# State-space sums in four row strips with a bank each, and means of q's squares as rows in four column strips

## The chip, the cores and the metric

One core of one Trainium2 chip (trn2) runs the kernel. The metric is the time of one execution on the device in microseconds, the median over several runs. The kernel drives five engines that run their own instruction streams and meet only at semaphores: TensorE (PE, matrix products into PSUM), VectorE (DVE), ScalarE (ACT), GpSimd (POOL) and SyncE (SP, which loads the weights). PSUM has eight banks of 128 partitions x 512 f32 here, `bank0` to `bank7`.

## The reference

Three blocks in a row work on x, 512 tokens of 1024 features. The first two are alike (attention over chunks, a convolution, retention, then an MLP of 4096). The third, the "second layer" of the names, has differential attention of 8 heads beside a state-space branch:

```python
xn = rmsnorm(h, norm1_gain[i])
proj = xn @ w_in[i]
q, k, v, u, gates = jnp.split(proj, splits, axis=-1)
q = rope(rmsnorm(q, q_norm_gain[i]), cos, sin)      # per head half of 64 features
k = rope(rmsnorm(k, k_norm_gain[i]), cos, sin)
...
# s5_layer: 32 groups of 16 channels, 64 complex states each
bu_re = jnp.einsum('blgc,gpc->blgp', uf, bb_re)
bu_im = jnp.einsum('blgc,gpc->blgp', uf, bb_im)
_, _, xr, xi = lax.associative_scan(_complex_affine_combine, (ar, ai, bu_re, bu_im), axis=1)
y = einsum(c_re, xr) - einsum(c_im, xi) + d_skip * uf
out = g * jax.nn.sigmoid(g @ w_glu + b_glu)         # g = gelu(y)
```

Only two parts of this third block matter here: the products that feed the scan of the states (sums over the channels), and the mean of the squares of q over each 64 features, which its norm needs.

## The kernel before

The residual x lies with features on partitions and tokens on the free axis. A weight matrix is streamed in units of 128 x 2048 values: SyncE loads a unit (`raw`), ScalarE rounds it to its high part (`w_hi`, line 1356), GpSimd makes the low part (`w_lo`, line 518), and TensorE does three products for each pair of tiles (high x high, high x low, low x high) at line 711. Two units are in flight at a time.

The projection of q and k in the second layer is cut into slots: one slot is 12 products of line 711 into one bank (0 to 3), and behind slot p TensorE runs `hook(p)`, small work for the state-space branch and the norms. Slots 0 to 15 make q (8 blocks of 128 features, two passes over four banks each), 16 to 31 make k, and v, the GLU and the projection follow. The other engines walk through the same numbers p in their own loops. The order is written out by hand in tuples of slots at lines 1270 to 1286. No planner moves anything: an engine does its instructions in this order and waits where a semaphore is not there yet.

The work that the change and the prediction touch:

- `sums_in(blk)` (line 999), hooks 8, 12, 16 and 20, for the four blocks of 128 channels. For each strip q of 32 partitions it multiplies `b_pow` by `uT`, over four sub-steps j and for a real and an imaginary part: 32 f32 products of 32 x 128 by 128 columns. The real part goes to bank 4, the imaginary part to bank 5, strip q to the columns q*128 of both. In a round r the real part takes strip r and the imaginary part strip r+1, so two strips are at work at once; three times per block TensorE waits until both strips are done (`strip_done`), so that no bank is written from two strips together.
- DVE, `states(blk, stage)` (line 2333), slots given by `STATES_AT`: stage 0 turns the sums (four reads of banks 4 and 5) and frees the two banks, stage 1 scans, stage 2 turns back and makes `state_ready`. It waits for tables that GpSimd makes (`turned`).
- `sums_out(blk)` (line 1017), hooks 14, 18, 22 and 26: products with `taps` (line 1024), then, when the state is ready, with the tables `ctab` (line 1031), all into bank 6, which DVE's `skip(blk)` reads and frees one slot later.
- `short_response` (line 987), hook 10: 32 products of line 995 into bank 6. ScalarE copies them to `taps` (line 1723).
- `q_columns(n)` (line 1035), hooks 9 and 17, for blocks 0 to 3 and 4 to 7 of q: the squares of q are the stationary operand, 128 tokens at a time, and two columns of `blk64` are the moving one, 16 products of 128 x 128 by 2 columns into bank 7. Tokens come out on partitions. DVE's `q_columns` (line 2376) adds the epsilon and frees bank 7; in slot 18 ScalarE and in slot 20 DVE (`column_root`) make the inverse root.
- In the same slots ScalarE takes q and k out of banks 0 to 3 with their squares (lines 1680 and 1682), and issues the DMAs that fetch each block's rotated partner, four per block (`fetch_partner`, line 1692, slots `PARTNER_AT`); DVE rotates (`rotate`, lines 2398 to 2401, slots `ROTATE_AT`: two blocks each in slots 8, 12, 16 and 20).
- `k_mean(j)` (lines 1051 and 1052, slots `K_AT` from 22 on) uses bank 7 in the same way for k, with ScalarE's `inverse_root` and DVE's `k_norm` behind it.

In DVE's loop one slot runs `skip`, then `states`, then its small jobs (rotations first). In ScalarE's loop it runs the next high part of weights (every fourth slot), the emptying of a bank, `short_response`, then the jobs, `fetch_partner` first.

## Time and profile of the kernel before

| what | value |
|---|---|
| median of 3 runs | 2146.66 us (2142.12 to 2146.75) |
| the profiled execution | 2144.72 us, its span 2142.9 us, granted clock 0.99 |
| TensorE products, busy | 2100.7 us, 98% of the span |
| VectorE / ScalarE / GpSimd busy | 1061.5 / 876.3 / 925.4 us |
| lines 1010 and 1041, the long forms of the change | 20.7 and 9.0 us busy |
| chain that ended last | PE 75%, issue 16%, POOL 3%, DVE 3% |

The span is what the profiler saw between the first and the last instruction; the time of the execution is 1.8 us longer. A f32 product leaves two records of TensorE, a product of line 711 one. "Granted clock" 1.00 is TensorE's full clock of 2.4 GHz, 0.50 the lower level of 1.2 GHz. Starts are in us from the start of the span. An engine that shows busy time beside another one's may still be what that one waits for: the timelines tell, not the shares.

### The profile page before, as it was taken

The page shows a single profiled execution, that of the slowest core. Times are in us where ns is not written, and L with a number is a line of the kernel's source. Part 1 is how long each engine was busy: PE and PEld are TensorE (multiplying, and loading weights), DVE is VectorE, ACT ScalarE, POOL GpSimd, SP SyncE. Part 2 cuts the span into 40 slices and gives each one's busy share as a digit, 9 for nine tenths or more (in the row PEclk, how much of TensorE's full clock was granted, in tenths as well). Part 3 has the DMA queues.
Part 4 walks back from the last instruction along what each step waited for, and adds up shares of the span by engine and source line. Part 5 has one row for each costly group of instructions (what it writes and reads, how often), then busy time and mean ns, then how long its engine had stood idle before and what let it go on. Part 6 is the DMA issues. An engine that isn't in the chain of part 4 may idle for free.

```text
span 2142.9 us, 27507 instructions
## 1 busy us (share of the span) xinstructions
PE 2100.7 (98%) x10200; PEld 1676.2 (78%) x10200; DVE 1061.5 (50%) x1725; ACT 876.3 (41%) x1219; POOL 925.4 (43%) x306
## 2 busy tenths in 40 slices
PE   8999999999999999999999999999999899999999
PEld 7875888888888776888888888877766787888887
DVE  5866242222247654422222258985588534554555
ACT  5345462223243445533222343164566534333332
POOL 5522444443455333545654456333312254444442
PEclk9999999999999999999999998899999999999999
DMA  5431213223224331233222242223111232322232
GB/s 182 150 117 71 77 63 98 97 98 98 99 69 149 125 93 46 79 99 98 94 100 87 92 148 85 66 84 108 60 60 60 95 100 81 97 88 90 97 98 78
DMA packets 120050, 202.29 MB, mean 94 GB/s; under 512 B 6544, under 2 KB 51856, under 8 KB 119696
## 3 DMA queue, kind: packets, MB, share of 16 engines
q1 hardware_dynamic: 112992, 189.12, 26.7%
q10 hardware_dynamic: 6960, 11.88, 1.9%
q8 instruction: 60, 0.98, 0.2%
q14 instruction: 38, 0.31, 0.0%
HBM read 189.44 MB, written 8.12 MB: 92 GB/s over the span
## 4 chain that ended last, share of the span: by engine, by line
PE 75%; issue 16%; POOL 3%; DVE 3%; ACT 1%; ACTq 1%; DMA 0%; POOLq 0%; DVEq 0%; SPq 0%
PE bank L711 63%; PE bank L813 5%; POOL w_lo L518 3%; PE bank L822 1%; PE bank L1010 1%; PE bank L765 1%; PE bank L840 1%; PE bank L880 1%; PE bank L774 1%; PE bank L868 0%; ACTq L1572 0%; DVE pr L2018 0%; PE bank L1041 0%; ACTq L1692 0%; PE bank L906 0%
## 5 line engine op out<-in xcount | busy, mean ns | idle before, releaser
L518 POOL TENSOR_TENSOR w_lo<-raw,w_hi 128x2048 fp32r<-128x2048 f32 (+1 forms) x167 | 741.9, 4442 | 1119.3 <-ACT w_hi L1356 1119.3
L711 PE MATMUL bank<-act_hi,w_hi 128*128 128x512 f32 x1488 | 595.6, 400 | 5.9 <-DVE hid L2561 2.5
L711 PE MATMUL bank<-act_hi,w_lo 128*128 128x512 f32 x1488 | 584.7, 393 | 0.0
L711 PE MATMUL bank<-act_lo,w_hi 128*128 128x512 f32 x1488 | 584.1, 393 | 0.0
L1356 ACT ACTIVATE w_hi<-raw 128x2048 fp32r<-128x2048 f32 (+1 forms) x170 | 314.2, 1848 | 591.2 <-PE bank L711 545.8
L711 PEld LDWEIGHTS bank<-act_hi,w_hi 128*128 128x128 f32 x1488 | 282.5, 190 | 78.0 <-issue 11.8
L711 PEld LDWEIGHTS bank<-act_hi,w_lo 128*128 128x128 f32 x1488 | 281.9, 189 | 60.7
L711 PEld LDWEIGHTS bank<-act_lo,w_hi 128*128 128x128 f32 x1488 | 282.5, 190 | 58.2 <-issue 1.4
L711 PE MATMUL bank<-h_hi,w_hi 128*128 128x512 f32 x704 | 277.7, 394 | 0.3 <-DVE x L2526 0.3
L711 PE MATMUL bank<-h_lo,w_hi 128*128 128x512 f32 x704 | 277.4, 394 | 0.0
L711 PE MATMUL bank<-h_hi,w_lo 128*128 128x512 f32 x704 | 277.4, 394 | 0.0
L2263 DVE TENSOR_TENSOR f<-f,bank 128x512 f32<-128x512 f32 x128 | 88.1, 688 | 238.7 <-PE bank L711 238.7
L2249 DVE SCALAR_TENSOR_TENSOR hid<-bank,rrow 128x512 f32<-128x512 f32 x64 | 43.7, 691 | 250.3 <-PE bank L711 245.3
L711 PEld LDWEIGHTS bank<-h_hi,w_hi 128*128 128x128 f32 x704 | 131.7, 187 | 33.4 <-DVE h_lo L2080 0.7
L711 PEld LDWEIGHTS bank<-h_hi,w_lo 128*128 128x128 f32 x704 | 131.7, 187 | 32.7
L711 PEld LDWEIGHTS bank<-h_lo,w_hi 128*128 128x128 f32 x704 | 131.7, 187 | 32.1
L2556 DVE TENSOR_TENSOR bank<-bank,rrow 128x512 f32<-128x512 f32 x44 | 30.7, 699 | 142.9 <-PE bank L711 140.4
L813 PE MATMUL bank<-act_hi,w_hi 128*128 128x512 f32 x192 | 76.3, 398 | 5.7 <-DVE act_lo L1940 5.2
L534 POOL TENSOR_TENSOR sums<-sums,squares 128x512 f32<-128x512 f32 x50 | 64.6, 1292 | 37.4 <-ACT squares L1374 35.1
L1993 DVE SCALAR_TENSOR_TENSOR bank<-ypad,lcol,bank 128x512 f32<-128x512 f32 x116 | 76.6, 755 | 0.0
L813 PE MATMUL bank<-act_hi,w_lo 128*128 128x512 f32 x192 | 74.8, 390 | 0.0
L813 PE MATMUL bank<-act_lo,w_hi 128*128 128x512 f32 x192 | 74.8, 389 | 0.0
(362 smaller groups left out, 2638.5 us busy)
## 6 DMA issues: line engine op xcount, KB each, us to landing
raw<-in_w_up SPq DMA_DIRECT2D x32, 1024.0 KB, 5.4
raw<-in_w_down SPq DMA_DIRECT2D x32, 1024.0 KB, 5.0
raw<-in_w_in SPq DMA_DIRECT2D x26, 1024.0 KB, 5.1
raw<-in_w_up SPq DMA_DIRECT2D x44, 512.0 KB, 4.6
raw<-in_w_in SPq DMA_DIRECT2D x28, 768.0 KB, 4.5
raw<-in_w_out SPq DMA_DIRECT2D x12, 1024.0 KB, 5.0
raw<-in_w_down SPq DMA_DIRECT2D x22, 512.0 KB, 4.2
raw<-in_w_attn_proj SPq DMA_DIRECT2D x4, 1024.0 KB, 5.1
```

The costliest lines, as they stand in the source:

```text
L518: pool.tensor_tensor(m.w_lo[slot][:, 0:n], m.raw[slot][:, 0:n], m.w_hi[slot][:, 0:n].bitcast(F32), ALU.subtract).then_inc(s["split_ready"], 1)
L534: ins = pool.tensor_tensor(m.sums[:], m.sums[:], m.squares[n % 4][:], ALU.add)
L711: mm = pe.matmul(o, ll if i == 2 else lh, rl if i == 1 else rh, start=first and n == 0, stop=last and n == len(steps) - 1)
L765: mm = pe.matmul(bank[b][:, t:t + 1], x[:, t * P:(t + 1) * P], m.per_d, start=(part == 0), stop=(part == 1))
L774: mm = pe.matmul(bank[b][:, t * P:(t + 1) * P], column[:, t:t + 1].to_broadcast([P, P]), m.ident, start=True, stop=True)
L813: mm = pe.matmul(bank[b][:], (wl if i == 2 else wh)[:, k % KU, cols], (m.act_lo if i == 1 else m.act_hi)[:, k, :], start=(k == 0 and i == ...
L822: pe.matmul(bank[b][:] if o is None else o, lhsT, rhs, start=True, stop=True).then_inc(s[f"full{b}"], 1)
L1356: act.activation(m.w_hi[slot][:, 0:n], m.raw[slot][:, 0:n], ACT.Copy).then_inc(s["w_hi"], 1)
L1993: ins = dve.scalar_tensor_tensor(to, y, w, sums, ALU.mult, ALU.add)
L2249: dve.scalar_tensor_tensor(m.hid[:, b, :], bank[b][:], 0.0, m.rrow[:], ALU.max, ALU.mult).then_inc(s[f"free{b}"], 1)
L2263: dve.tensor_tensor(sums, sums, bank[4 + b][:], ALU.add).then_inc(s[f"free{4 + b}"], 1)
L2556: dve.tensor_tensor(bank[b][:], bank[b][:], m.rrow[:], ALU.mult).then_inc(s["up_scaled"], 1)
```

## The change

`sums_in` now has four banks, 4 to 7, one for each strip, allocated as one tensor `quad`. The real part of strip q goes to columns 0 to 127 of bank 4+q, the imaginary part to columns 128 to 255. Four products of four different strips follow each other, and the waits for `strip_done` are gone. DVE's step 0 reads the four banks with one instruction for each of its four turns and frees all four at its end; one of these turns is now waited for.

The means of q's squares are made in two steps. `q_rows(n)` (hooks 10 and 18) takes 32 columns of `blk64` as the stationary operand and the squares as the moving one: four products of 512 columns, each to its strip of 32 partitions of bank 7. ScalarE copies the bank to `q_rows` in SBUF. `q_columns(n)` (hooks 11 and 19, instead of 9 and 17) turns that by four products with picked columns of the identity. `COLUMN_ROOT_AT` goes from 18 to 20. The number of f32 products falls from 2 x 16 to 2 x (4 + 4) there and stays 4 x 32 in `sums_in`.

```diff
--- before.py
+++ after.py
@@ -188,7 +188,9 @@
 
     with ExitStack() as ctx:
         m = memory(nc)
-        m.bank = [ctx.enter_context(nc.psum_tensor(f"bank{i}", [P, T], F32)) for i in range(8)]
+        m.bank = [ctx.enter_context(nc.psum_tensor(f"bank{i}", [P, T], F32)) for i in range(4)]
+        m.quad = ctx.enter_context(nc.psum_tensor("bank4", [P, 4, T], F32))
+        m.bank += [m.quad[:, i, :] for i in range(4)]
         m.x_park = nc.dram_tensor("x_park", (P, NT * D), F32, kind="Internal").ap()
         m.bias_table = nc.dram_tensor("bias_table", (DEPTH, 6, P * N_BIAS), F32, kind="Internal").ap()
         s = {name: ctx.enter_context(nc.semaphore(name)) for name in SEMAPHORES}
@@ -227,7 +229,7 @@
     "bias_loaded",
     "table_loaded",
     "x_parked", "x_back",
-    "taps_clear", "u_ready", "strip_done", "spread", "kernel_made", "glu_done",
+    "taps_clear", "u_ready", "spread", "kernel_made", "glu_done",
     "arena_free",
     "w_loaded0", "w_loaded1",
     "w_hi",
@@ -370,6 +372,7 @@
     m.partner = [ar(f"partner{i}", [P, T], 68 + 2 * i) for i in range(2)]
     m.q_root = [ar(f"q_root{i}", [P, T], 72 + 2 * i) for i in range(2)]
     m.q_mean, m.q_power = (ar(name, [P, 2, 8, NT], 72 + 2 * i) for i, name in enumerate(("q_mean", "q_power")))
+    m.q_rows = ar("q_rows", [P, T], 92)
     m.g_hi, m.g_lo = (ar(f"gated{i}", [P, 4, T], 76 + 8 * i, F32R) for i in range(2))
     m.uT = put("uT", [P, 4, T], at=late_at)
     m.ssm = ar("ssm", [P, KD, T], 40)
@@ -998,21 +1001,18 @@
 
     def sums_in(blk):
 
-        fill(4)
-        fill(5)
+        for b in QUAD:
+            fill(b)
         if blk == 0:
             pe.wait_ge(s["u_ready"], 4)
             pe.wait_ge(s["param_dve"], N_PARAM_B)
-        for r in range(4):
+        for part in range(2):
             for j in range(SUB):
-                for part in range(2):
-                    q = (r + part) % 4
-                    mm = pe.matmul(bank[4 + part][:, q * P:(q + 1) * P], m.b_pow[strips[q], SUB - 1 - j, part, blk, :],
+                for q, b in enumerate(QUAD):
+                    mm = pe.matmul(bank[b][:, part * P:(part + 1) * P], m.b_pow[strips[q], SUB - 1 - j, part, blk, :],
                                    m.uT[strips[q], blk, j * N_SUB:(j + 1) * N_SUB], start=(j == 0), stop=(j == SUB - 1))
-                    if j == SUB - 1:
-                        mm.then_inc(s["strip_done" if r < 3 else f"full{4 + part}"], 1)
-            if r < 3:
-                pe.wait_ge(s["strip_done"], c.up("strip_done", 2))
+                    if part == 1 and j == SUB - 1:
+                        mm.then_inc(s[f"full{b}"], 1)
 
     def sums_out(blk):
 
@@ -1032,14 +1032,20 @@
                                    start=False, stop=(part == 1), skip_group_check=True)
         mm.then_inc(s["full6"], 1)
 
-    def q_columns(n):
+    def q_rows(n):
 
         pe.wait_ge(s["q_squared"], c.up("q_squared", 4))
         fill(7)
         for j in range(4):
-            for t in range(NT):
-                mm = pe.matmul(bank[7][:, 0:8 * NT].rearrange("p (c j t) -> p c j t", c=2, t=NT)[:, :, j, t], m.q_square[j][:, t * P:(t + 1) * P],
-                               m.blk64.rearrange("p (c d) -> p c d", c=2)[:, :, 0], start=True, stop=True)
+            mm = pe.matmul(bank[7][strips[j], :], m.blk64.rearrange("p (c d) -> p c d", d=4)[:, :, 0], m.q_square[j][:], start=True, stop=True)
+        mm.then_inc(s["full7"], 1)
+
+    def q_columns(n):
+
+        fill(7)
+        for t in range(NT):
+            mm = pe.matmul(bank[7][:, 0:8 * NT].rearrange("p (c j t) -> p c j t", c=2, t=NT)[:, :, :, t], m.q_rows[:, t * P:(t + 1) * P],
+                           m.ident.rearrange("p (j c d) -> p c j d", j=4, c=2)[:, :, :, 0], start=True, stop=True)
         mm.then_inc(s["full7"], 1)
 
     def k_mean(j):
@@ -1061,6 +1067,8 @@
                 sums_in(blk)
             if p == SUMS_OUT_AT[blk]:
                 sums_out(blk)
+        for n in jobs_at(p, ROWS_AT):
+            q_rows(n)
         for n in jobs_at(p, COLUMNS_AT):
             q_columns(n)
         for j in jobs_at(p, K_AT):
@@ -1267,7 +1275,8 @@
     return x[:, 0, :], x[:, 1, :]
 
 
-COLUMNS_AT, COLUMN_ROOT_AT = (9, 17), 18
+QUAD = (4, 5, 6, 7)
+ROWS_AT, COLUMNS_AT, COLUMN_ROOT_AT = (10, 18), (11, 19), 20
 K_AT = (22, 24, 26, 28, 30, 36, 38, 42)
 PARTNER_AT = (6, 7, 10, 10, 14, 15, 18, 18, 21, 22, 24, 26, 29, 34, 36, 40)
 ROTATE_AT = (8, 8, 12, 12, 16, 16, 20, 20)
@@ -1703,6 +1712,8 @@
 
         for j in jobs_at(p, PARTNER_AT):
             fetch_partner(j)
+        for n in jobs_at(p, ROWS_AT):
+            evac(7, m.q_rows[:])
         for n in jobs_at(p, COLUMNS_AT):
             use(7)
         if p == COLUMN_ROOT_AT:
@@ -1739,7 +1750,7 @@
         if p == SHORT_AT:
             short_response()
         if p in SUMS_IN_AT:
-            use(4, 5)
+            use(*QUAD)
         if p in SUMS_OUT_AT:
             use(6)
         jobs(p)
@@ -2336,16 +2347,18 @@
         sin, cos = m.sin_n[blk % 2][:], m.cos_n[blk % 2][:]
         if stage == 0:
             dve.wait_ge(s["turned"], blk + 1)
-            full(4)
-            full(5)
-            dve.tensor_tensor(w0, bank[4][:], cos, ALU.mult).then_inc(s["dve_step"], 1)
-            dve.tensor_tensor(w2, bank[4][:], sin, ALU.mult).then_inc(s["free4"], 1)
+            for b in QUAD:
+                full(b)
+            re, im = (m.quad[:, :, part * P:(part + 1) * P] for part in range(2))
+            by_strip = lambda x: x.rearrange("p (q n) -> p q n", q=4)
+            dve.tensor_tensor(by_strip(w0), re, by_strip(cos), ALU.mult).then_inc(s["dve_step"], 1)
             c.up("dve_step")
-            link(dve.tensor_tensor(w1, bank[5][:], sin, ALU.mult))
+            dve.tensor_tensor(by_strip(w2), re, by_strip(sin), ALU.mult)
+            link(dve.tensor_tensor(by_strip(w1), im, by_strip(sin), ALU.mult))
             link(dve.tensor_tensor(w0, w0, w1, ALU.add))
-            dve.tensor_tensor(w1, bank[5][:], cos, ALU.mult).then_inc(s["free5"], 1)
-            freed(4)
-            freed(5)
+            link(dve.tensor_tensor(by_strip(w1), im, by_strip(cos), ALU.mult))
+            for b in QUAD:
+                dve.sem_inc(s[f"free{b}"], 1)
             link(dve.tensor_tensor(w1, w1, w2, ALU.subtract))
         if stage == 1:
             for q in range(4):
@@ -2412,6 +2425,8 @@
 
         for j in jobs_at(p, ROTATE_AT):
             rotate(j)
+        for n in jobs_at(p, ROWS_AT):
+            use(7)
         for n in jobs_at(p, COLUMNS_AT):
             q_columns(n)
         if p == COLUMN_ROOT_AT + 2:
```

## Rows read from the trace of the kernel before

**Rows 1.** The page of the kernel before, its first part: busy time of each engine.

```profile
PE 2100.7 (98%) x10200; PEld 1676.2 (78%) x10200; DVE 1061.5 (50%) x1725; ACT 876.3 (41%) x1219; POOL 925.4 (43%) x306
```

**Rows 2.** Windows: length, busy us of each engine (instructions), granted clock, DMA share, GB/s.

```profile
1290.00:1405.00 115.00, 113.89 (x901) 93.83 (x900) 101.53 (x125) 28.23 (x38) 59.69 (x30) 0.88 0.25 74
...
1302.60:1307.40 4.80, 4.80 (x14) 3.80 (x13) 4.77 (x2) 0.00 (x0) 4.80 (x3) 0.54 0.11 17
...
1319.00:1324.50 5.50, 5.50 (x24) 4.34 (x24) 2.89 (x5) 2.37 (x4) 0.00 (x0) 1.00 0.15 36
...
1357.40:1362.00 4.60, 4.60 (x12) 3.60 (x13) 4.53 (x4) 0.00 (x0) 4.44 (x4) 0.54 0.25 61
```

**Rows 3.** Timeline of TensorE, 1296 to 1407: start, length, line, operation, records.

```profile
1296.73 5.93 PE L1010 MATMUL bank<-uT,b_pow 32*128 32x128 f32 x64
...
1307.48 4.15 PE L1041 MATMUL bank<-cmat,q_square 128*128 128x2 f32 x32
...
1316.89 2.09 PE L995 MATMUL bank<-ctab,braw 128*32 128x128 f32 x64
...
1324.58 4.92 PE L1010 MATMUL bank<-uT,b_pow 32*128 32x128 f32 x64
...
1335.00 2.39 PE L1024 MATMUL bank<-uT,taps 128*128 128x128 f32 x20
...
1352.57 4.80 PE L1041 MATMUL bank<-cmat,q_square 128*128 128x2 f32 x32
...
1371.98 6.08 PE L1010 MATMUL bank<-uT,b_pow 32*128 32x128 f32 x64
...
1389.66 1.12 PE L1051 MATMUL bank<-q_square,cmat 128*128 128x512 f32 x2
...
1405.99 1.52 PE L1031 MATMUL bank<-state,ctab 128*32 128x128 f32 x48
```

**Rows 4.** Line 1010: what ended TensorE's idle time before it (us, times).

```profile
  PE bank L1010: 3.6, 12
```

**Rows 5.** Timeline of VectorE (DVE), 1299 to 1405; in brackets its idle time before.

```profile
1299.65 0.86 DVE L2398 TENSOR_TENSOR partner<-partner,rope 128x512 f32<-128x512 f32 x1 [3.59 <-DMA partner<-q]
...
1301.15 4.91 DVE L2401 TENSOR_TENSOR q<-q,partner 128x512 f32<-128x512 f32 x1
...
1310.70 0.69 DVE L2341 TENSOR_TENSOR w<-bank,cos_n 128x512 f32<-128x512 f32 x1
...
1313.34 0.69 DVE L2346 TENSOR_TENSOR w<-bank,cos_n 128x512 f32<-128x512 f32 x1
...
1325.61 0.69 DVE L2398 TENSOR_TENSOR partner<-partner,rope 128x512 f32<-128x512 f32 x1 [3.65 <-DMA partner<-q]
...
1328.18 0.69 DVE L2398 TENSOR_TENSOR partner<-partner,rope 128x512 f32<-128x512 f32 x1 [0.55 <-DMA partner<-q]
...
1334.53 0.69 DVE L2341 TENSOR_TENSOR w<-bank,cos_n 128x512 f32<-128x512 f32 x1
...
1338.86 5.25 DVE L2355 TENSOR_TENSOR_SCAN w<-par,w 128x128 f32<-128x128 f32 x8
...
1361.50 0.69 DVE L2341 TENSOR_TENSOR w<-bank,cos_n 128x512 f32<-128x512 f32 x1
...
1382.70 0.69 DVE L2341 TENSOR_TENSOR w<-bank,cos_n 128x512 f32<-128x512 f32 x1
...
1387.23 2.63 DVE L2355 TENSOR_TENSOR_SCAN w<-par,w 128x128 f32<-128x128 f32 x8
...
1404.26 0.69 DVE L2366 TENSOR_TENSOR state<-state,w 128x508 f32<-128x508 f32 x1
```

**Rows 6.** Timeline of ScalarE (ACT), around hook 10; ACTq is its issuing of DMAs.

```profile
1319.13 2.44 ACT L1723 ACTIVATE taps<-bank 32x512 f32<-32x512 f32 x4 [18.27 <-PE bank L995]
1321.68 5.01 ACTq L1692 DMA_DIRECT2D partner<-q  x8
```

**Rows 7.** Timeline of GpSimd (POOL): the low parts of one unit of weights.

```profile
1328.78 5.17 POOL L518 TENSOR_TENSOR w_lo<-raw,w_hi 128x2048 fp32r<-128x2048 f32 x1 [14.33 <-ACT w_hi L1356]
```

## Prediction

> **What bounds the kernel now.** I read the page first. TensorE is busy for 98% of the span [rows 1], so a change that makes its work shorter looks like a gain of the same size. That is an average, so I then read the stretch that the change touches, second layer, hooks 8 to 26, 1290 to 1405 us: by the windows its granted clock is 0.88 against 1.00 around it, TensorE is busy for 113.9 of 115 us and VectorE (DVE) for 101.5 [rows 2]. Next the timeline of TensorE in it: four `sums_in` of 4.9 to 6.1 us and two `q_columns` of 4.2 and 4.8 us [rows 3]. Last the timelines of DVE, ScalarE and GpSimd [rows 5 to 7]. The reader is to see there that DVE works nearly without a gap from 1299.65 to 1405: it idles 3.65 and 0.55 us for partners of q [rows 5], and in those 105 us does the rotations of q and the three steps of `states` for four blocks, in an order written out by hand. The last of these, the state of block 3, is done at 1404.95 (1404.26 and 0.69), and the products of `sums_out(3)` that read it start at 1405.99 [rows 3, 5]. So TensorE is 98% busy, and DVE is one microsecond behind it at the end of this stretch. What TensorE saves ahead of 1405 is worth about 1 us unless DVE gets shorter too.
>
> **What TensorE saves by itself.** A slot of 12 `L711` products takes 2.75 us at full clock (24 in 5.5) and 4.6 to 4.8 in windows at a mean clock of 0.54 [rows 2].
> `sums_in`: 32 products, 64 records. Before, two strips ran at once, and three times per block the strips waited for each other: 3.6 us over 12 waits [rows 4], 0.9 a block. Now four strips in four banks. The nearest row is `L995`, 64 records of the same 128 columns, four tiles side by side (column strips), in 2.09 us [rows 3]. The bounds are 2.1 and 4.0 (two at a time as before, less the 0.9 of waits). I take 2.1, because `L995` has the same shape and number of records. Four blocks cost 5.93 + 4.92 + 4.92 (the third is like the second) + 6.08 = 21.9 us, and then 8.4: 13.5 saved.
> A rule of the Trainium skill says the same with another size (TensorE: Matmul & The Clock Gate, "Measured speedup vs the span model"): four row tiles gave 3.07 times, not 4. A full-width product is 0.24 us here (`L1024`, 10 in 2.39) [rows 3]; by that rule 32 would take an estimated 2.5 us. The sum does not need it.
> `q_columns`: 16 products in 4.15 and 4.80 become 4 `q_rows` of 512 columns and 4 turning products. One 512-column f32 product takes 1.12 [rows 3]; four in column strips take 1.1 if side by side, 4.3 if one after another. I take 1.1 (`L995` again shows column strips side by side). Four turning products at 4.15/16 = 0.26 are 1.04. Twice: 8.95 becomes 4.3, 4.7 saved.
> Clock: the granted clock falls to its lower level (1.2 GHz) in or right behind both long forms, while TensorE worked in narrow strips or on 2-column products, and the slots behind run at half, as behind the first `sums_in` and behind the second `q_columns` [rows 2]. The two long forms of 5.93 and 6.08 stand beside two of 4.92, and both `q_columns` are followed by slow slots, so I count four such events: about 2 us each, 8 in all. Both forms get short, so this goes too.
> Together 13.5 + 4.7 + 8 = 26 us, if nobody else were late.
>
> **What is late next.** The four sums now take banks 4 to 7, and all four come free only after DVE's step 0 of `states` has read them. Banks 6 and 7 had nothing to do with that before. Queued behind on TensorE: `short_response` (hook 10) and `sums_out` (14, 18, 22), which fill bank 6, and `q_rows`, which fills bank 7. Times are on the clock of the old trace.
> Hook 10. TensorE is there at 1296.73 + 2.1 + 2 x 2.75 = 1304.3. DVE has two rotations before `states(0,0)`, which starts at 1310.70; nothing of these hangs on the sums (partner transfers, and GpSimd's instruction that holds DVE for 4.91 instead of 0.69) [rows 5]. The last bank is read by the instruction at 1313.34, so they come free at 1314.1. TensorE idles 9.8 us. It starts `short_response` at 1314.1 instead of 1316.89 [rows 3]: 2.8 us are left of the gain so far.
> Hook 11. The turning products wait for ScalarE's copy of bank 7, which stands behind the four copies of the taps (2.44) and, in the same slot, eight issues of partner transfers (5.01) [rows 6]. `short_response` ends at 1316.2 (1317.5 if at half clock: I take 3.4 for 2.1, as its columns then take twice the time), + 0.1 + 2.44 + 0.1 + 5.01 + 0.6 for the copy (a quarter of the taps' row) = 1324.5 to 1325.8. `q_rows` and a slot would be over at 1320 to 1323, so TensorE waits again. Turned at 1325.6 to 1326.9, next slot done at 1328.4 to 1329.7, `sums_in(1)` starts there, against 1324.58: the gain is gone. Its 2.1 against 4.92 brings it back to 1330.5 to 1331.8 against 1329.5 [rows 3].
> DVE then. It now takes the column means after `states(0,2)` and ahead of rotation 2, which thus starts at 1326.0 to 1327.2 instead of 1325.61 [rows 5]: +0.4 to +1.6, I take +0.5. `states(1,0)` follows: +0.5, starting at 1335.0. The banks are free 3.4 us later, 1338.4 (1313.34 + 0.69 - 10.70 of rows 5). TensorE reaches `sums_out(0)` at 1336 to 1337.3, waits, and starts it some 3.4 us later than the 1335.00 of before.
> From here each block has one loop: `states(k,0)` starts, 3.5 us later `sums_out(k-1)` may start, it takes 4.4 (`L1024` 2.39 and 64 records of `L1031` of the shape of `L995`, 2.0), and DVE's `skip` reads it 7.9 us after the start. DVE gets there after 4.3 us of step 0 (1334.53 to 1338.86) and a scan of 2.63, or 5.25 when GpSimd works beside it [rows 5]: 7.0 to 9.6. So it idles 0 to 1 us in each of blocks 1 to 3: +1.0 in all. If TensorE stands at half clock after its idle time, `sums_out` takes up to 7.8 and DVE idles up to 3.4 more. Two of these could be hit; I put +1 for it.
> Saved on this path: DVE's short idle of 0.55 goes: -0.5. The added `link` and the four-bank form of four reads cost 4 x 0.1 at the names of `states`, by the same elements as before: between 0 and 4 x 4 x 0.1 = 1.6; I take 0, because 512 columns take 0.69 from either bank and from SBUF [rows 5].
> Sum at the state of block 3: +0.5 + 1.0 + 1.0 - 0.5 = +2.0 us. The starts of `states` (1334.53, 1361.50, 1382.70) and the end (1404.95) should all move by 0 to +3. Behind 1405 nothing is changed, so the shift goes through to the end. Profiled execution: 2144.7 + 2.0 = 2146.7 (its span is 2142.9, 1.8 lie around it). The median of the runs, 2146.7, is 1.9 above that execution, so I forecast 2146.7 + 2.0 = 2148.7.
> A rule of the Trainium skill speaks against this change in just this way (TensorEngine Tiling, "PSUM Bottleneck"): tiling speeds up TensorE and not the emptying of the banks, which may then bind. The row that bears on it is the one microsecond at 1405.
>
> **GpSimd as a source of spread.** Each of its `L518` instructions holds back a DVE instruction whose operands both come from SBUF: 4.91 for 0.69 [rows 5], beside `L518` of 5.17 us [rows 7]. One stands in the stretch for every four slots. ScalarE now issues its parts at other times, so one may miss DVE or hit it twice: 4.2 us to either side.
>
> **Rivals.** (A) The gain comes through: 2146.7 - 26 = 2121. It needs DVE to lose 26 us of its 105. For it: TensorE's 98%. Against it: DVE's rows; none of DVE's work is removed. Chance 0.05. (A') A part comes through: DVE's collisions with GpSimd fall away one to three times: 2148.7 less 4.2 to 12.6, 2144.5 to 2136.1, I say 2140. Chance 0.10. (B) Slower: the idle times in hooks 10, 11, 14 and 18 keep TensorE at its lower clock when it has just been released, and now exactly that work, `sums_out`, is what DVE waits for. Price 3.4 us a block, decided by whether the clock is at half when the banks come free; with three blocks and the slot behind hook 11 (+1.7) it gives +2.0 - 1 + 10.2 + 1.7 = +12.9, 2160; with two blocks and without the slot 2146.7 + 1 + 6.8, some 2155, and 2157 with one small term of 2 more. For it: the clock fell within the two long forms and an idle engine does less than they did. Against it: DVE often gets to `skip` late by itself. Chance 0.23. (C) The four strips don't run side by side (4.0 in place of 2.1 a block, `q_rows` 4.3). TensorE then comes to hooks 14, 18 and 22 up to 1.9 us later, where it waits 1 to 7 us anyway: +0 to +2, 2150. Chance 0.08; same side as the forecast.
>
> **How the numbers follow.** Forecast 0.54 at 2148.7, its own range 2144.5 to 2153; C 0.08, A 0.05, A' 0.10, B 0.23. To hold 8 in 10 the range leaves out A and the outer part of B: from one collision less with no other cost (2148.7 - 4.2 - 2.5, the three added terms, is 2142; I say 2141.5) to B with two blocks (2157). What can be told from no change is 0.3%, 6.4 us: faster means below 2140.3, slower above 2153.1. Faster: A and a half of A', 0.10. Slower: all but 0.01 of B, 0.22. Same: 0.68.
>
> **What would show it.** In the trace after: `sums_in` 64 records in about 2.1 us (2.5 to 4 would be C); TensorE idle near 10 us ahead of `L995` and 2 to 4.5 ahead of the turning products, with DVE and ScalarE as releasers; `sums_out` starting right after the last bank read of `states`, four times; DVE's `skip` with idle time ahead of it; the granted clock low behind the waits, not behind the sums; the end of `states(3,2)` at 1405 to 1408. If TensorE does not wait at hook 10, or `states(3,2)` ends before 1400, the prediction is wrong in its main step.

## The result, and the profile after

The changed kernel is slower, by about half of one per cent: 2156.9 us, median of 6 runs (2153.2 to 2159.6), against 2146.7 (2142.1 to 2148.7), ratio 1.0054 with an interval of 1.0043 to 1.0066 (a ratio stands with its 95% interval here and below). Its profiled execution took 2156.95 us, its span was 2155.1, 12.2 longer than the old span of 2142.9. The forecast was 2148.7 and "the same"; the time lies at the very edge of the range and on the side of rival B.

First the page of the kernel after: the busy line, and the shares of the chain that ended last.

```profile
PE 2088.1 (97%) x10168; PEld 1665.3 (77%) x10168; DVE 1061.5 (49%) x1725; ACT 876.7 (41%) x1221; POOL 924.2 (43%) x306
PE 74%; issue 15%; DVE 5%; POOL 3%; ACT 1%; DMA 1%; ACTq 1%; DVEq 0%; POOLq 0%
```

TensorE's busy time fell by 12.6 us against [rows 1] and the kernel got 10 us longer; DVE's is the same to a tenth. So the question is what TensorE waits for. The waits of TensorE over the whole kernel (who waits, for whom: us in total, times, longest) are led by three that the kernel before does not have:

```profile
PE bank L1024 <- DVEq L2361: 12.6, 3, 6.3
PE bank L998 <- DVEq L2361: 8.0, 1, 8.0
...
PE bank L1047 <- ACT q_rows L1370: 4.3, 1, 4.3
```

`L1024` is `sums_out`, `L998` is `short_response` (L995 before), `L1047` the turning products; `L2361` is the place where DVE frees the four banks of `quad`, `L1370` ScalarE's copy of the rows. That is 24.9 us of new waits in five places. Now the timeline of TensorE, with the idle time before each piece of work in brackets. `L1012` is `sums_in` (L1010 before), `L1040` `q_rows`.

```profile
1299.63 2.07 PE L1012 MATMUL bank<-uT,b_pow 32*128 32x128 f32 x64
...
1315.37 3.64 PE L998 MATMUL bank<-ctab,braw 128*32 128x128 f32 x64 [8.00 <-DVEq L2361]
...
1318.78 1.37 PE L1040 MATMUL bank<-q_square,cmat 128*32 128x512 f32 x8
...
1327.38 1.88 PE L1047 MATMUL bank<-cmat,q_rows 128*128 128x8 f32 x8 [4.29 <-ACT q_rows L1370]
...
1333.89 2.07 PE L1012 MATMUL bank<-uT,b_pow 32*128 32x128 f32 x64
...
1345.55 3.57 PE L1024 MATMUL bank<-uT,taps 128*128 128x128 f32 x20 [3.93 <-DVEq L2361]
...
1371.17 3.86 PE L1024 MATMUL bank<-uT,taps 128*128 128x128 f32 x20 [6.33 <-DVEq L2361]
...
1394.41 4.13 PE L1024 MATMUL bank<-uT,taps 128*128 128x128 f32 x20 [2.39 <-DVEq L2361]
...
1414.37 2.39 PE L1024 MATMUL bank<-uT,taps 128*128 128x128 f32 x20
```

The sums take 2.07 instead of 4.92 to 6.08, as meant. But everything that stands right behind a wait takes up to twice its time: 3.64 for the 2.09 of [rows 3], and `sums_out`'s `L1024` 3.57, 3.86 and 4.13 for 2.39. The windows of three such places show the clock (columns as in [rows 2]: length, busy us of each engine, granted clock, DMA share, GB/s); 0.50 is 1.2 GHz:

```profile
1315.37:1318.80 3.43, 3.43 (x68) 3.17 (x72) 3.27 (x5) 0.00 (x0) 2.50 (x2) 0.50 0.02 5
1345.50:1349.10 3.60, 3.55 (x24) 3.33 (x28) 3.33 (x9) 0.00 (x0) 0.00 (x0) 0.67 0.12 28
1394.30:1398.50 4.20, 4.09 (x24) 3.97 (x26) 3.83 (x12) 0.00 (x0) 0.00 (x0) 0.59 0.25 62
```

Then ScalarE around hook 11: the copy of the rows, at the end of this fence, stands behind the taps and the eight issues of partner transfers, as in [rows 6].

```profile
1319.13 2.44 ACT L1734 ACTIVATE taps<-bank 32x512 f32<-32x512 f32 x4 [14.39 <-PE bank L998]
1321.68 5.00 ACTq L1701 DMA_DIRECT2D partner<-q  x8
1326.73 0.60 ACT L1370 ACTIVATE q_rows<-bank 128x512 f32<-128x512 f32 x1 [5.16 <-issue]
```

Last DVE, from the column means (`L2394`) on: rotations 2 and 3 (`L2411` to `L2414`), `states(1,0)` (`L2354`), the scan, and `skip` (`L2384`); and the end of the last state.

```profile
1329.38 0.19 DVE L2394 SCALAR_TENSOR_TENSOR q_mean<-small,bank 128x32 f32<-128x32 f32 x1 [4.98 <-PE bank L1047]
1329.71 4.60 DVE L2411 TENSOR_TENSOR partner<-partner,rope 128x512 f32<-128x512 f32 x1
1334.23 1.54 DVE L2413 TENSOR_TENSOR q<-q,rope 128x512 f32<-128x512 f32 x1
...
1338.87 1.54 DVE L2413 TENSOR_TENSOR q<-q,rope 128x512 f32<-128x512 f32 x1
...
1341.91 0.69 DVE L2354 TENSOR_TENSOR w<-bank,cos_n 128x512 f32<-128x512 f32 x1
...
1346.40 2.63 DVE L2368 TENSOR_TENSOR_SCAN w<-par,w 128x128 f32<-128x128 f32 x8
...
1351.69 0.75 DVE L2384 SCALAR_TENSOR_TENSOR uT<-uT,scol,bank 128x512 f32<-128x512 f32 x1 [2.65 <-PE bank L1031]
...
1404.03 0.69 DVE L2084 SCALAR_TENSOR_TENSOR q_square<-bank,q_square 128x512 f32<-128x512 f32 x1 [3.34 <-ACT q_square L1377]
...
1414.74 0.69 DVE L2379 TENSOR_TENSOR state<-state,w 128x508 f32<-128x508 f32 x1
```

DVE now idles 4.98 us for the means, 2.65 and (at the second `skip`) 0.82 for `sums_out`, and 3.34 for a square of k. Behind the last bank read of step 0 (`L2359`) DVE stands still for 0.43 us in each of the four blocks, where it did so once, for 0.46, in the profile of before:

```profile
1345.68 0.69 DVE L2362 TENSOR_TENSOR w<-w,w 128x512 f32<-128x512 f32 x1 [0.43 <-DVE w L2359]
```

Of the 12.2 us, 2.9 arise ahead of the change: the first sums start at 1299.63, against 1296.73 [rows 3]; over all the profiles of this case that start lies between 1296.2 and 1301.9. So from here on I count from the first product of the sums, so that nothing ahead of them enters. These are the starts of `states(k,0)` and the end of the last state, read from the timelines of DVE, with the medians and ratios of all runs:

| kernel | states 0, 1, 2, 3 start | last state ends | ratio to before |
|---|---|---|---|
| before | 14.0, 37.8, 64.8, 86.0 | 108.2 | |
| after | 11.9, 42.3, 67.7, 91.1 | 115.8 | 1.0054 [1.0043, 1.0066] |

The starts of a kernel come from its one profiled execution, which was the fastest of its runs for `e3`, `e4`, `e7` and `e9` below and the slowest for `e5` and `n1`. The loss of 7.6 us in the stretch has its largest part between the first and the second `states`: 30.3 us instead of 23.8. The first start is 2.0 earlier, the second to third 1.5 shorter, the third to fourth 2.2 longer, the rest 2.4 longer. The remaining 1.7 of the 12.2 lie behind the stretch, where nothing is changed.

DVE's own account of the stretch, from the same two timelines: it idles 20.3 us instead of 12.0. Its 17 instructions that take longer than their usual time (0.69 us; 2.63 for a scan), all of them beside one of GpSimd's, take 29.5 us too much instead of 31.2. So the collisions moved and did not grow; what grew is the idle time. Of the 8.3 us more, 3.5 are `skip` waiting for `sums_out`, 1.7 a square of k, 1.6 the partner of the rotation at 1360.19, 0.9 the short stops behind `L2359`, and 0.8 that it waits for the means (4.98) in place of two partners (3.65 and 0.55); the start of the stretch takes back 0.2.

### The profile page after: what moved, and what is told of

Same layout as the page of the kernel before. It is cut to its first block, busy times and chain, and to the rows that moved or that the text cites. A ratio compares the mean times of both kernels' runs of the same rounds, so it can differ in the third digit from the quotient of the medians.

```text
span 2155.1 us, 27464 instructions
## 1 busy us (share of the span) xinstructions
PE 2088.1 (97%) x10168; PEld 1665.3 (77%) x10168; DVE 1061.5 (49%) x1725; ACT 876.7 (41%) x1221; POOL 924.2 (43%) x306
## 4 chain that ended last, share of the span: by engine, by line
PE 74%; issue 15%; DVE 5%; POOL 3%; ACT 1%; DMA 1%; ACTq 1%; DVEq 0%; POOLq 0%
PE bank L714 62%; PE bank L816 5%; POOL w_lo L521 3%; PE bank L825 1%; DVE q L2413 1%; PE bank L768 1%; PE bank L883 1%; PE bank L843 1%; PE bank L871 1%; PE bank L1024 1%; ACTq L1701 1%; DVE partner L2411 0%; PE bank L777 0%; PE bank L792 0%; DVE pr L2029 0%
```

## Experiments

### Both kernels a second time

No edit; the two kernels as they are, for how far one profile is to be trusted.

> The kernel before once more, for a second profile: how much of the first one's stretch (108.2 us from the first sums to the last state, with 27.3 us at the lower clock) is the kernel's and how much is that one execution's. Theory 4 (the long forms bring the clock down only when they happen to fill the stretch it is judged on, so an execution can have few or many such events): another time at the lower clock, 7 to 20 us, and a stretch of 103 to 107 us. Otherwise both repeat.

> The changed kernel once more. Theory 1: the waits of TensorE repeat within 1 us (8 at hook 10, 4.3 for the copy, 12 ahead of L1024), since they hang on orders written out by hand; the stretch of 115.8 us repeats within 2. Theory 4: only the time at the lower clock moves.

Measured: 2151.9 and 2160.4 us, one run each. After repeats itself: the starts are 12.2, 42.3, 68.0, 92.4 and the end 117.0, with `L998` waiting 8.3, `L1047` 4.6 and `L1024` 13.3. Before repeats to 0.1 us up to the third start (13.9, 37.8, 64.7), then 86.9 and 111.2. DVE's account repeats in kind: 14.9 us idle in before and 21.4 in after, 31.3 and 29.6 us too much in the held instructions. The granted clock of the stretch differs, though. The windows of 1290 to 1405 us: of this repeat, and, of a kernel with the same work on TensorE (before without rotations of q, below):

```profile
1290.00:1405.00 115.00, 113.88 (x880) 93.44 (x880) 98.55 (x121) 28.55 (x39) 59.26 (x30) 0.85 0.24 72
```

```profile
1290.00:1405.00 115.00, 113.88 (x1005) 93.59 (x1004) 84.47 (x110) 31.90 (x45) 58.75 (x30) 0.99 0.29 84
```

0.88 in [rows 2], 0.85 and 0.99 here. The windows don't hold the same work (901, 880 and 1005 records). Taken from the first sums to the end of the last state, they hold 871, 870 and 872 records of the same products in the same order, in 108.2, 111.2 and 97.4 us, at a clock of 0.87, 0.85 and 0.98. So the low clock of the stretch in one profile is no fixed property of its two long forms. The third is another kernel on DVE, and why its clock stayed up is not shown.

The runs on record give a wider view. Before was timed again beside the experiments, 91 runs in all: their granted clock over the whole execution lies between 0.983 and 0.995 and their time between 2155.7 and 2137.2 us, longer where the clock is lower. At 0.987 and 0.988 twelve runs of before took 2145.0 to 2151.1 us, and four of the six runs of after 2156.8 to 2158.1. So at the same mean clock most of the loss is still there, and more time at the low clock in all can be only the smaller part of it. Where in the execution the low clock stands, this mean does not tell.

### Each part alone

`e1_sums_only`: the four-bank sums, with the column means as before.

```diff
-    def q_rows(n):            # its hook, ScalarE's copy and its use on DVE go too
-            mm = pe.matmul(bank[7][strips[j], :], ...m.blk64..., m.q_square[j][:], ...)
     def q_columns(n):
+            for t in range(NT):   # the 16 products of before, at hooks 11 and 19
+                mm = pe.matmul(bank[7][...][:, :, j, t], m.q_square[j][:, t * P:(t + 1) * P], ...)
```

> The sums in four strips with a bank each as in the changed kernel; the means of q's squares in the long form of before (16 products), at hooks 11 and 19, with no copy by ScalarE. Theory 1 (the four banks are held until VectorE has read them, so short_response and sums_out wait for VectorE; the q part costs little): TensorE waits 8 us at hook 10 and 4 to 6 us at hooks 14 and 18 as in the changed kernel; the copy's wait of 4.3 us goes, 2 x 3 us of longer products come. VectorE's column means come at about 1324 (on the clock of the changed kernel) instead of 1329.4, rotation 2 with them. Time 2 to 5 us below the changed kernel, 2152 to 2155. Theory 2 (the means part, by its copy behind the DMA issues, is what costs): all of the loss goes, 2147 or less.

Measured: 2148.5 us (10 runs), ratio 1.0016 [0.9997, 1.0034]; starts 12.2, 36.1, 59.7, 85.3, end 109.4. Its waits of TensorE:

```profile
PE bank L998 <- DVEq L2351: 8.2, 1, 8.2
PE bank L1024 <- DVEq L2351: 7.2, 2, 5.8
```

`e2_means_only`: before, with the new column means alone (the sums keep `bank[4 + part]` and `strip_done`).

> The sums as before (two strips, banks 4 and 5); the means as rows with ScalarE's copy and the four turning products, at the changed kernel's hooks. Theory 1: bank 6 and 7 are free when TensorE gets there, nothing waits for VectorE's states; short_response comes about 5 us earlier than before, the partner transfers with it, so rotation 2 starts 2 to 4 us earlier and the path through VectorE gets shorter by that: 3 us below before, 2143 to 2145. Theory 2: the wait for the copy (about 4 us at hook 11) and what follows make it slower than before, 2150 to 2155.

Measured: 2144.1 us (10 runs), ratio 1.0000 [0.9984, 1.0015]; starts 13.9, 38.7, 62.2, 82.9, end 103.9. The wait for the copy is there too, and hardly another:

```profile
PE bank L1048 <- ACT q_rows L1370: 4.6, 1, 4.6
```

What follows: the sums alone bring the waits for DVE's banks but only about a third of the loss, and the interval reaches below 1. Taking the new means away thus gave back some 8 us, not the 2 to 5 that I expected of it, which is closer to theory 2. The means alone cost nothing, as expected under theory 1. Together they cost 0.54%. The two are not a sum of parts: with the banks of two strips `short_response` does not wait, ScalarE gets to taps, issues and copy sooner, and the 4.6 us of the copy end in time for DVE (its `states(1,0)` is 0.9 late against 4.5).

### The copy ahead of the DMA issues

One edit on ScalarE, made to the changed kernel (`e4_copy_first`) and to `e2` (`e9_means_copy_first`, and once more as `e12_means_copy_first_again`):

```diff
+        for n in jobs_at(p, ROWS_AT):
+            evac(7, m.q_rows[:])
         for j in jobs_at(p, PARTNER_AT):
             fetch_partner(j)
-        for n in jobs_at(p, ROWS_AT):
-            evac(7, m.q_rows[:])
```

> The changed kernel with ScalarE's copy of bank 7 ahead of the issues of the partner transfers in the same slot. Theory 1: the wait ahead of the turning products (4.3 us) goes, the column means come 5 us earlier, but rotation 2 still waits for its partner, some 0.6 us later than in the changed kernel: starts 1326 to 1327 instead of 1329.7; 2 to 4 us below the changed kernel, 2153 to 2155. If the waits for the banks were not what costs, it would give back 5 us or more.

Measured: 2150.5 us (7 runs), ratio 1.0029 [1.0018, 1.0041]; starts 12.1, 35.1, 60.6, 85.0, end 109.6. `e4`'s ScalarE, and DVE's means and the last rotation before `states(1,0)`:

```profile
1318.45 0.60 ACT L1370 ACTIVATE q_rows<-bank 128x512 f32<-128x512 f32 x1
1318.48 5.00 ACTq L1701 DMA_DIRECT2D partner<-q  x8
```

```profile
1321.59 0.19 DVE L2394 SCALAR_TENSOR_TENSOR q_mean<-small,bank 128x32 f32<-128x32 f32 x1 [0.43 <-PE bank L1047]
...
1326.32 4.98 DVE L2414 TENSOR_TENSOR q<-q,partner 128x512 f32<-128x512 f32 x1
1331.33 0.69 DVE L2354 TENSOR_TENSOR w<-bank,cos_n 128x512 f32<-128x512 f32 x1
```

The copy's wait is gone, DVE's idle of 4.98 is 0.43, and 0.25% of the 0.54% with it, about 5.4 us. I had expected 2 to 4, and had written that 5 or more would speak against the waits for the banks as what costs. The waits for the four banks stay, 8.2 for `L998` and 11.6 in three for `L1024`, and so does the other half of the loss; that the one makes the other is argued, not shown.

> The sums as before, the means as rows, and ScalarE's copy of bank 7 ahead of the issues of the partner transfers. The wait of 4.6 us for the copy at hook 11 goes. Theory 1: VectorE's path is what sets the end of the stretch, and rotation 2 waits for its partner as before, so little comes of it: 0 to 2 us below the run with the means alone, 2142 to 2144. Theory 2 (TensorE's waits are the loss one for one): 4 to 5 us below it, 2140 or less.

> The means as rows with ScalarE's copy first and the sums as before, once more with more rounds. Theory 1 (VectorE near the bound of the stretch, TensorE saves 4 us in it by the means and the transfers of partners 2 and 3 start earlier): 0 to 3 us below the kernel before, a difference at the edge of what can be measured; all theories expect no loss.

Measured: 2142.8 (10 runs), ratio 1.0001 [0.9990, 1.0012], and 2143.5 (11 runs), ratio 0.9989 [0.9979, 1.0000]; ends 101.3 and 102.4. Both end the stretch 6 to 7 us ahead of the profile of before, and the medians do not show it. This is the best version of the means, and I can't tell it from the kernel before.

### DVE in another order

`e3_turn_sums_first`: `states(0,0)` ahead of the first two rotations of q, so that the banks come free early. `e5_both_orders` has the edit of `e4` as well.

```diff
-ROTATE_AT = (8, 8, 12, 12, 16, 16, 20, 20)
+ROTATE_AT = (9, 9, 13, 13, 17, 17, 21, 21)
```

> The changed kernel with one tuple changed: VectorE rotates q one slot later (9, 13, 17, 21), so that it turns the sums and frees the four banks before the two rotations of that slot. Theory 1: the waits ahead of L998 (8.0 us) and ahead of L1024 (12.6 us in three) fall to under 6 us in all; 6 to 10 us below the changed kernel, 2147 to 2151, no further because VectorE's own work of some 100 us stays. Theory 3 (VectorE's order does not matter, only the lower clock and GpSimd's collisions): within 3 us of the changed kernel.

> The changed kernel with both orders changed: VectorE's rotations of q one slot later, behind step 0 of the states, and ScalarE's copy of bank 7 ahead of the issues of partner transfers. With the rotations later the partners of blocks 2, 3 and 6, 7 are fetched later and the copy stood behind them (10.5 us of waits in the run with the rotations alone moved); the copy first takes that away. Theory 1: all waits of TensorE in the stretch under 8 us, the last state 100 to 106 us after the first sums; 3 to 8 us below the kernel before, 2137 to 2142. If collisions with GpSimd rule: 2145 to 2150.

Measured: 2152.9 us (4 runs), ratio 1.0050 [1.0034, 1.0067], and 2153.5 (5 runs), ratio 1.0048 [1.0031, 1.0064]. The states start early (3.4 and 3.3) and it buys nothing; I had expected 2147 to 2151 and 2137 to 2142. The first wait of each list, of `e3` and of `e5`:

```profile
PE bank L1047 <- ACT q_rows L1370: 10.5, 2, 6.5
```

```profile
PE bank L1012 <- DVE q_mean L2394: 23.7, 2, 14.3
```

In `e3` the copy is waited for longer. In `e5` the copy is in time, but DVE takes the column means out of bank 7 only behind its rotations and states; until then the next sums, which need bank 7 as one of their four, stand still for 14.3 us. I had not seen this and expected the gain. Bank 7 is thus the second coupling that the four banks bring.

Two more orders on top of `e5`: `e10_means_taken_first` takes the means between `skip` and `states`, `e11_short_early` has `short_response` at hook 5 besides, ahead of the sums.

```diff
-        for n in jobs_at(p, COLUMNS_AT):
-            q_columns(n)
     ...                       # skip
+        for n in jobs_at(p, COLUMNS_AT):
+            q_columns(n)
```

```diff
+        pe.wait_ge(s["table_loaded"], 4 * 16)
-SHORT_AT = 10
+SHORT_AT = 5
```

> The kernel with both orders changed, and VectorE taking the column means ahead of the state's last step instead of behind rotations and states. There TensorE waited 23.7 us ahead of the sums for VectorE to free bank 7. Theory 1 (a bank that is held by VectorE's order is what costs): the wait falls to under 10 us, the time from 2153.5 to 2143 to 2147, about the kernel before. If it stays over 2150, the order of the means isn't it.

> The same with short_response at hook 5, ahead of the first sums, so that bank 6 isn't asked for at hook 10 and ScalarE's taps are out of the way. Theory 1: the wait at hook 10 stays only as far as bank 7 is not free (0 to 3 us); TensorE saves by itself, so the stretch is 98 to 104 us and the time 2 to 6 us below the kernel before, 2138 to 2142. Below that it can't get, as VectorE's own work is about 95 us.

Measured: 2148.2 us, ratio 1.0007 [0.9990, 1.0023], and 2148.2, ratio 1.0008 [0.9987, 1.0028], 10 runs each. From `e5` to `e10` one thing is changed, when DVE empties bank 7: the waits of the sums for `q_mean` fall from 23.7 us to 2.3, and the ratio from 1.0048 to 1.0007, although the waits ahead of `L998` and `L1024` grow from 2.6 to 14.2 us. This is the plainest test here that a bank held by DVE's order costs time, and also that not every microsecond of such waits does. The loss is gone and no gain is in its place; I had expected a gain of `e11`. In `e11` `short_response` no longer waits at hook 10, but `q_rows` (`L1041` there) does in its stead, for bank 7, 2.7 us against 3.6 in `e10`; and 10.6 us of `L1025` (`sums_out`) remain in three waits, as many as in `e10`. Two lines of `e11`'s list:

```profile
PE bank L1025 <- DVEq L2362: 10.6, 3, 4.5
...
PE bank L1041 <- DVEq L2362: 2.7, 1, 2.7
```

### Without rotations of q

The test that I meant for the main claim, that DVE's queue is what bounds the stretch: the same edit to before (`e7`) and to after (`e8`) leaves out the 24 rotation instructions of q, some 17 us of DVE at 0.69 each. The waits for the partners' transfers stay in.

```diff
         wait(f"partner{j % 2}", 4 * 16)
+        if j < KD:
+            dve.sem_inc(s["q_ready"], 1)
+            c.up("q_ready")
+            return
```

> The kernel before without VectorE's rotation of the eight blocks of q (24 instructions left out, so q is not rotated; k is). Theory 1 (in the stretch from the first sums to the last state VectorE is within 1 us of being the bound, TensorE the bound up to there): TensorE has no waits to lose there, so the time falls by 0 to 3 us only, 2142 to 2145.

> The changed kernel without the same 24 instructions. Theory 1: VectorE frees the four banks in time, the waits ahead of L998 and L1024 go, only the copy's wait at hook 11 stays, and what TensorE saves by itself comes through: 12 to 22 us below the kernel before without rotation, 2122 to 2132. Theory 3 (what costs is in TensorE itself, the strips or the lower clock, not VectorE): it stays near the changed kernel, 2150 or more.

Measured: before without rotations 2142.0 us, ratio 1.0000 [0.9987, 1.0013]; after without them 2143.6, ratio 1.0004 [0.9990, 1.0019], 10 runs each; the ends of the last state are 97.4 and 101.2. That before stays the same, as I expected, is what a kernel bound by TensorE would do. That after does not fall to 2122 to 2132 contradicts my expectation: with DVE lighter the loss goes, but not one of TensorE's saved microseconds comes out. The waits say where they are:

```profile
PE bank L1012 <- DVE q_mean L2394: 5.5, 1, 5.5
PE bank L1047 <- ACT q_rows L1370: 4.5, 1, 4.5
...
PE bank L998 <- DVEq L2361: 2.6, 1, 2.6
...
PE bank L1024 <- DVEq L2361: 2.3, 1, 2.3
```

14.9 us of waits, all for banks 4 to 7 or the copy. So DVE's amount of work is not the whole bound: the chain sums, step 0, taps, copy, turning, means, next sums is a ring through the four banks, and it stays when DVE is lighter. The test is not a pure one, though. DVE still stands before two of its four `states` for a partner, while the finished sums lie in the four banks for 2.7 and 1.5 us of that time:

```profile
1304.46 0.69 DVE L2354 TENSOR_TENSOR w<-bank,cos_n 128x512 f32<-128x512 f32 x1 [5.48 <-DMA partner<-q]
...
1347.75 0.69 DVE L2354 TENSOR_TENSOR w<-bank,cos_n 128x512 f32<-128x512 f32 x1 [4.20 <-DMA partner<-q]
```

How much of the 14.9 us would be left without these stops was not tried.

### Without GpSimd's tables of blocks 2 and 3

The new late `states(1,0)` puts rotations 2 and 3 beside GpSimd's turn tables of block 2. `n1` (before) and `n2` (after) leave them out and use those of blocks 0 and 1.

```diff
             pool.wait_ge(s["state_ready"], 2 * (b - 1))
+            pool.sem_inc(s["turned"], 1)
+            return
```

> The kernel before without GpSimd's six instructions for the turn tables of blocks 2 and of 3 (the tables of blocks 0 and 1 are read in their place, so the states of blocks 2 and 3 are wrong). Theory 1 and 5 (5: GpSimd's instructions hold back VectorE's and this is part of what costs): VectorE's rotations 4 and 5 (8.3 us) fall to about 4, the scan of block 1 from 5.25 to 2.6; TensorE had no waits, so 0 to 2 us below the kernel before.

> The changed kernel without the same twelve instructions. Theory 5: rotations 2 and 3 take 8 to 9 us instead of 12.2, the scan of block 2 2.6 instead of 3.6; the last state 109 to 112 us after the first sums instead of 115.8, the time 4 to 7 us below the changed kernel, 2150 to 2153. Theory 1 without 5 (only the later start and the waits for banks count): it stays within 2 us of the changed kernel.

Measured: 2143.6 us (10 runs), ratio 0.9991 [0.9976, 1.0007], and 2152.4 (7 runs), ratio 1.0025 [1.0012, 1.0037]. Rotations 2 and 3 of `n2`, first and last but one of six:

```profile
1330.25 4.62 DVE L2413 TENSOR_TENSOR partner<-partner,rope 128x512 f32<-128x512 f32 x1
...
1336.84 0.68 DVE L2415 TENSOR_TENSOR q<-q,rope 128x512 f32<-128x512 f32 x1
```

They take 8.0 us, against 12.2 in after, where the last five are 1.43 to 1.67 each. From the first to the second `states` is 25.7 us in `n2`, against 30.3. The time of `n2` is as I expected. Its ratio is 0.29% below that of after; against `n1`, its proper partner, 0.34% are left of the 0.54%. The difference of 0.2% or 4 us is the size of the collision's price by the medians, but the three intervals together leave it uncertain by about as much. It acts in the same interval as the copy; whether the two gains add was not tried.

### The price of a wait in clock

No kernel of its own: the 20 products of `sums_out` over uT and the taps (`L1024` in after), in the timelines of TensorE of all the kernels here, sorted by the idle time before them (us).

| idle before | how often | took |
|---|---|---|
| none | every other time, in every kernel | 2.39 or 2.40 |
| 0.16 to 2.60 | 7 | 2.50 each |
| 2.30 to 2.39, all before the third `sums_out`, in e4, n2, after and its repeat | 4 | 3.36, 3.48, 4.13, 3.46 |
| 3.01 to 6.58 | 12 | 3.57 to 4.64 |

Each wait of 3 us and more is followed by 1.2 to 2.2 us of extra work at the lower clock; of the shorter ones only those of a third `sums_out` whose second had already run slow. This is a correlation over 23 waits and no edit of the clock, but it holds in kernels with different orders.

## Why the prediction was wrong, point by point

**What bounds the kernel.** Half right. TensorE's 12.6 us less brought nothing, as said, and the reader of 98% would have been misled. But "DVE is one microsecond behind" was read as a bound by DVE's amount of work; `e8` shows that this is not the whole of it: without a sixth of DVE's work in the stretch after gains no more than its loss. `e7` alone would fit either reading. And of the 96 us that DVE is busy in the stretch of before, 31 are what its held instructions take too long, so its amount of work was not fixed either.

**What TensorE saves.** The sums 2.07 (2.1 said), `q_rows` 1.37 and 1.04 (1.1), the turning 1.88 and 0.95 (1.04). Rival C fell with the first. The 8 us of clock were taken from one execution: the same work shows 0.85, 0.87 and 0.98 of the clock in three, so this term was no fixed property of the two forms. It stood only in the 26 us of TensorE and not in the forecast. The estimate by the Trainium skill (TensorE: Matmul & The Clock Gate, "Measured speedup vs the span model"), 2.5 for the sums by its 3.07 times, was above the measured 2.07 (32 products at 0.24 are 7.7, and 7.7/2.07 is 3.7 times).

**Waits.** All five stand where they were named. Hook 10: 8.0 us, said 9.8. `short_response` 3.64 at half clock, said 3.4. Turning: 4.3, said 2 to 4.5. With the shift of 2.9 taken off, rotation 2 starts at 1326.8, inside the 1326.0 to 1327.2 said, so `states(1,0)` is 1.2 late by this, in place of the +0.5 that I took.

**The step that failed: what DVE meets behind rotation 2.** `states(1,0)` was put at +0.5 and came at +4.5. 1.2 is the copy; the other 3.3 are rotations 2 and 3, 12.2 us against 8.9 (1325.61 to 1334.53 in [rows 5]), beside GpSimd's tables of block 2. I had named GpSimd as a spread of 4.2 to either side, by its large instruction; the small ones, 1.4 to 1.7 for 0.69 five times over, were in no term. Part came back: the scan took 2.63 instead of 5.25 [rows 5]. It was no help, since `skip` then idled 2.65 for `sums_out`. Over the whole stretch the collisions cost no more than before (29.5 us against 31.2): they say where the 4.5 arose, not why the end is late. What the sum of +2.0 had wrong is DVE's idle time, which grew by 8.3 us. The largest term is the next one, put at +1.0 and +1.0. The stops behind `L2359`, 0.9 in sum, stand where step 0 now frees its banks by four instructions of their own; I had put the new form of step 0 at 0. And the wait of 1.6 for a later partner was in no term.

**The loop of three blocks.** Skip's idle was put at +1.0 and half clock at +1.0. `sums_out` stood at low clock in all three blocks, 1.2 to 1.7 us more each, 4.4 in sum, not in two of them with a small effect. DVE idled 2.65 and 0.82 at `skip`, and 3.34 for k's square against 1.63 in the profile of before. That is rival B's mechanism. It is cheaper than its 3.4 a block: I had 7.8 for `sums_out` at half clock, and the one of hook 14 took 6.0 (1345.55 to 1351.52). The idle time at these three places is 5.2 us more than before, against the 2.0 that I had put. 2.6 of it can be set against what the scan had given back; how much of it is the lower clock and how much the later banks, these rows don't separate. Its chance of 0.23 was too low: three waits of several microseconds stood in my own sum, and [rows 2] showed that the clock falls easily here.

**Rivals A and A'.** Fell; nothing came through, not even in `e8`. The copy as a lever was seen as a wait of TensorE only; `e4` shows that its turn behind eight issues carried about half of the loss. It takes away TensorE's wait and DVE's idle time together; but `e2` has the same wait of TensorE (4.6 us) and loses nothing, so the way through DVE's means is the likelier one.

**The rule that spoke against the change** (the Trainium skill, TensorEngine Tiling, "PSUM Bottleneck") agrees with the sign. How it comes about here: the emptying did not get slower (0.69 us for four banks' columns at once), but four banks stay taken until the last of four reads, and other work needs two of them.

**What stays open.** How much of DVE's idle time comes from `sums_out` at the lower clock and how much from its late banks: both are in each run, and no edit sets the clock. The 1.7 us behind the stretch: I did not test them. Whether `e9`/`e12` beat before: the one interval is 0.9979 to 1.0000, the other 0.9990 to 1.0012. And why 4 to 7 us less in the stretch, by the profiles of `e2`, `e9` and `e12`, don't reach the medians: their clock (0.94 in `e9`, against 0.88) may be the draw of one execution. For it: `e9`'s profiled execution took 2139.8 us at 0.992 over the whole, where eight runs of before took 2137.4 to 2143.3. Splitting `quad` into pairs of banks that are freed after each read, or sums that avoid banks 6 and 7, was not tried.

## What to carry to other kernels

Each strip took a bank of its own here. Before counting the saving, list for every added bank who else uses it, who empties it and when. Put the next user's wait in the sum, and a second, smaller term for the work right behind it, which took 1.2 to 2.2 us longer for 2.39 behind the waits of 3 us and more here. Then ask who waits for that work in turn. A small copy that a product waits for belongs ahead of DMA issues in its engine's program order; here that order was worth 0.25% in the changed kernel, and nothing that could be measured with the sums as before. Moving a late engine's work also moves what it runs beside, so look at the neighbours at the new place.

## What the runs showed of the hardware

- Four row strips with a bank each ran 64 records of 128 columns in 2.07 us, the same with two at a time 4.92 to 6.08. One DVE instruction that reads 128 columns from each of four banks takes 0.69, as one of 512 columns from a single bank.
- A DVE instruction whose operands all come from SBUF took up to 5.1 us in place of 0.69 beside GpSimd's weight instructions (4.6 to 5.1 in the stretches of before and after), and 1.4 to 1.7 beside its small table products. Those of 512 columns that read a bank stayed at 0.69 to 0.75 in each timeline, also where the ones before and behind them were held.
- The same products in the same order, 870 to 872 records, took 97.4, 108.2 and 111.2 us at a granted clock of 0.98, 0.87 and 0.85 (the first in the kernel without rotations of q). One kernel, before, had 0.983 to 0.995 over the whole execution in 91 runs, and 2155.7 to 2137.2 us.
